# Level matmuls of the gated recurrence: 64 moving columns, one bank per chunk and level, two levels in four banks

## What is computed

```
def step(state, xs):                      # one chunk of 128 tokens
    qc, kc, vc, lfc = xs
    cb = jnp.cumsum(lfc, axis=1)
    rel = cb[:, :, None] - cb[:, None, :]
    dec = jnp.where(causal, jnp.exp(jnp.where(causal, rel, 0.0)), 0.0)
    a = jnp.einsum('bqhd,bkhd,bqkhd->bhqk', qc, kc, dec)
    o = jnp.einsum('bhqk,bkhe->bqhe', a, vc) + jnp.einsum('bqhd,bhde->bqhe', qc * jnp.exp(cb), state)
    ...
```

## Time and profile before

| | |
|---|---|
| time, median of 3 runs | 3101.59 us (3099.38 to 3101.69) |
| the profiled execution | 3100.82 us, its span 3099.0 us |
| TensorE's granted clock, mean over the span | 0.982 |
| TensorE busy | 95% of the span, 21052 matmul passes |
| weight loads busy | 86% |
| VectorE, ScalarE, GpSimd busy | 55%, 43%, 13% |

### The profile page before, as it was taken

The page is one execution under the profiler, slowest core; times in us unless marked ns, Lnnn a source line. Parts: engine busy times, 40 slices in busy tenths (PEclk is TensorE's granted clock), DMA queues, the critical chain, the costliest instruction groups (busy, mean ns, idle before and its releaser), DMA issues. The chain is left out here.

```text
span 3099.0 us, 54135 instructions
## 1 busy us (share of the span) xinstructions
PE 2951.6 (95%) x21052; PEld 2664.4 (86%) x21052; DVE 1717.1 (55%) x2483; ACT 1344.3 (43%) x1856; POOL 398.7 (13%) x306
## 2 busy tenths in 40 slices
PE   5999998999999999999899999999999998999998
PEld 2667765677999999899899989799999998988998
DVE  2223224276555556655445865657845577565784
ACT  1222213135544444544444544456644453536663
POOL 2111000122111110211100110101101002020110
PEclk8999999999999999999999999999999999999999
DMA  8986353841555654465435405245555451433564
GB/s 296 285 256 191 106 168 112 219 138 55 169 178 149 183 178 143 148 182 178 138 122 169 145 28 177 69 139 148 171 161 157 141 164 37 151 108 109 149 181 132
DMA packets 586161, 474.88 MB, mean 153 GB/s; under 512 B 28720, under 2 KB 547888, under 8 KB 585664
## 3 DMA queue, kind: packets, MB, share of 16 engines
q1 hardware_dynamic: 584464, 460.44, 48.7%
q0 software_dynamic: 1520, 11.95, 1.3%
HBM read 471.23 MB, written 4.72 MB: 154 GB/s over the span
## 5 line engine op out<-in xcount | busy, mean ns | idle before, releaser
L2213 DVE TENSOR_TENSOR low<-raw,high 128x1024 fp32r<-128x1024 f32 (+1 forms) x744 | 911.0, 1227 | 826.2 <-ACT high L2013 818.4
L2013 ACT CAST high<-raw 128x1024 fp32r<-128x1024 f32 (+1 forms) x744 | 767.9, 1033 | 1080.5 <-PE PS L1925 797.2
L1923 PE MATMUL PS<-NHh,high 128*128 128x272 f32 (+1 forms) x2304 | 669.2, 290 | 14.2 <-DVE NHl L1725 4.7
L1925 PE MATMUL PS<-NHh,low 128*128 128x272 f32 (+1 forms) x2304 | 661.1, 287 | 0.0
L1924 PE MATMUL PS<-NHl,high 128*128 128x272 f32 (+1 forms) x2304 | 660.2, 287 | 0.0
L1923 PE MATMUL PS<-XH,high 128*128 128x256 f32 (+1 forms) x1856 | 587.6, 317 | 28.3 <-issue 14.4
L1924 PE MATMUL PS<-XL,high 128*128 128x256 f32 (+1 forms) x1856 | 579.8, 312 | 0.0
L1925 PE MATMUL PS<-XH,low 128*128 128x256 f32 (+1 forms) x1856 | 579.6, 312 | 0.0
L1923 PEld LDWEIGHTS PS<-NHh,high 128*128 128x128 f32 x2304 | 433.4, 188 | 19.5 <-issue 15.4
L1924 PEld LDWEIGHTS PS<-NHl,high 128*128 128x128 f32 x2304 | 434.0, 188 | 0.8
L1925 PEld LDWEIGHTS PS<-NHh,low 128*128 128x128 f32 x2304 | 433.6, 188 | 0.0
(11 more groups left out here) (328 smaller groups left out, 4070.6 us busy)
## 6 DMA issues: line engine op xcount, KB each, us to landing
raw<-w_in_dram SPq DMA_DIRECT2D x416, 256.0 KB, 3.1
raw<-ffn_w_in_dram SPq DMA_DIRECT2D x352, 256.0 KB, 3.2
part<-ada_w_dram SPq DMA_DIRECT2D x184, 256.0 KB, 4.2
raw<-w_ffn_in_dram SPq DMA_DIRECT2D x176, 256.0 KB, 3.2
raw<-ffn_w_out_dram SPq DMA_DIRECT2D x160, 256.0 KB, 3.1
raw<-w_branch_dram SPq DMA_DIRECT2D x96, 256.0 KB, 3.2
raw<-w_ffn_out_dram SPq DMA_DIRECT2D x80, 256.0 KB, 3.0
part_sg<-ada_w_dram SPq DMA_DIRECT2D x48, 256.0 KB, 3.0
```

The lines of the kernel that those rows point to most:

```text
L1923: nc.tensor.matmul(out, wh, xh, start=(k0 + k == 0), stop=False)
L1925: last = nc.tensor.matmul(out, wl, xh, start=False, stop=(c == len(kch) - 1 and k == nk - 1))
L2013: nc.scalar.copy(high[:, slot, 0:nk, :], raw[:, slot, 0:nk, :]).then_inc(s_high, 1)
L2213: nc.vector.tensor_tensor(low[:, slot, 0:nk, :], raw[:, slot, 0:nk, :], high[:, slot, 0:nk, :].bitcast(F32), ALU.subtract).then_inc(s_low, 1)
```

## The change

A level's matmul keeps its 128 weight columns (all tokens of the chunk), but its moving operand is the right halves alone: `right_half(x, s)` takes s columns, leaves s out, and so on, 64 in all. The result is written without gaps, 64 values per head, so eight heads fill one bank of 512 values instead of two. Chunk c of level n now lies in bank 2 (n mod 2) + c: even levels in banks 0 and 1, odd levels in banks 2 and 3. So a chunk's bank was last used two levels below, and the wait on `s_hk` asks for the pick of chunk c of level n - 2 instead of n - 1. The pick reads its source without gaps and writes into `AM` as before. For the last chunk of 16 tokens the matmuls stay as they are, and the pick takes the right halves of what they wrote.

```diff
--- before.py
+++ after.py
@@ -1132,9 +1132,9 @@
                     last = nc.tensor.matmul(out, lhs[:, h, t0:t0 + wd], rhs[:, h, t0:t0 + wd], start=True, stop=True)
             return last
 
-        def level_banks(n, c):
-
-            return 2 * (c % 2)
+        def level_bank(n, c):
+
+            return 2 * (n % 2) + c
 
         def small_bank(n):
             return 4 if n % 2 else 5
@@ -1147,10 +1147,11 @@
                 for h in range(HH):
                     nc.tensor.matmul(PS[0:wd, small_bank(n), h * wd:(h + 1) * wd], q[:, h, t0:t0 + wd],
                                      q[:, h, t0:t0 + wd], start=True, stop=True)
-            t = slice(c * P, (c + 1) * P)
+            s, half = LEVELS[n], P // 2
             for h in range(HH):
-                last = nc.tensor.matmul(PS[:, level_banks(n, c) + h // 4, (h % 4) * P:(h % 4 + 1) * P],
-                                        q[:, h, t], q[:, h, t], start=True, stop=True)
+                x = q[:, h, c * P:(c + 1) * P]
+                out = PS[:, level_bank(n, c), h * half:(h + 1) * half].rearrange("p (b t) -> p b t", t=s)
+                last = nc.tensor.matmul(out, x, right_half(x, s), start=True, stop=True)
             return last
 
         def right_half(ap, s):
@@ -1171,7 +1172,7 @@
                     early(1)
                 pe.wait_ge(s_hq, NL * layer + n + 1)
                 for c in range(2):
-                    pe.wait_ge(s_hk, NPICK * layer + max(1, 2 * n + c))
+                    pe.wait_ge(s_hk, NPICK * layer + max(1, 2 * n + c - 2))
                     hg_level(n, c).then_inc(s_ht, 1)
             early(2)
             pe.wait_ge(s_hk, NPICK * (layer + 1))
@@ -1417,15 +1418,15 @@
                 dve.wait_ge(s_ht, t + 2 * n + c + 2)
                 dve.wait_ge(s_hk, NPICK * layer + 2 * n + c + 1)
                 s, m = LEVELS[n], C2["levels"] + (n + 1) * P
-                parts = [(c * P, P, PS[:, level_banks(n, c):level_banks(n, c) + 2, :])]
+                parts = [(c * P, P, PS[:, level_bank(n, c), :].rearrange("p (h b t) -> p h b t", h=HH, t=s))]
                 if c and s <= 8:
                     t0, wd = CHUNKS[2]
-                    parts.append((t0, wd, PS[0:wd, small_bank(n):small_bank(n) + 1, 0:HH * wd]))
+                    src = PS[0:wd, small_bank(n), 0:HH * wd].rearrange("p (h t) -> p h t", t=wd)
+                    parts.append((t0, wd, right_half(src, s)))
                 for t0, wd, src in parts:
-                    src = src.rearrange("p a (h t) -> p (a h) t", t=wd)
                     mask = con2[0:wd, m:m + wd].bitcast(I32)
                     last = nc.vector.copy_predicated(right_half(AM[0:wd, :, t0:t0 + wd], s),
-                                                     bc(right_half(mask, s), HH), right_half(src, s))
+                                                     bc(right_half(mask, s), HH), src)
                 last.then_inc(s_hk, 1)
 
             def end_exponents():
```

## The result

The changed kernel took 3117.18 us (median of 4 runs, 3115.23 to 3124.44), the kernel before 3101.16 beside it (4 runs, 3099.38 to 3101.69): ratio 1.0057, 95% interval 1.0039 to 1.0074. It is slower by 16 us, 2.6 times the 6.2 us (0.2%) that can be told from no change. The profiled run took 3115.23 with a span of 3113.4, 14.4 us over that of before.

What follows compares the result with a forecast made beforehand. TensorE (busy 95%) bounds the kernel, with levels 2 to 4 paced by GpSimd and VectorE. Profiled 3100.82 + 8.5 (layer 0) + 12.5 (layer 1) = 3121.8, given as 3122 us; own range 3113 to 3131, 8-in-10 range 3101 to 3131.

Steps and rivals of the forecast that it cites:

- The removed wait, worth nothing: Second chunk of a level no longer waits for the pick one level below; no TensorE wait named a pick: nothing.
- 64 columns gain TensorE nothing: Level matmuls: the weights' load sets the pace, so a 64-column pass stays at 0.1125 us at full clock.
- the third rival: Columns set the pace, about 0.06 us a pass, and the clock holds: 3.7 us gained per layer, 3093.4 us; chance 0.06.
- The strides at nothing: Level matmuls: reading the moving operand in strides was costed at nothing.
- Picks 0.5 us shorter on the path: Level 1's first pick, reading PSUM contiguously, gets shorter: -0.5 us per layer, bounds 0 and -0.6.
- The clock falls in levels 2 to 5 and comes back in the chunk after level 6: Each layer: TensorE drops to half clock somewhere in those levels, returning only in the merge-gate chunk after level 6.
- Price 0.22 a pass, 7.06 a level: At half clock a 64-column pass costs 0.22 us, and a level of 32 passes 7.06 us.
- Layer 0, +8.5: Layer 0 with the fall in mid level 3: +8.8 to the transposes, -1.3 in them, net +7.5; +8.5 taken.
- the 1.0 that I had added for an earlier fall: Layer 0: net +7.5 was raised to +8.5, as a fall one chunk earlier adds 2.0.
- Layer 1, +12.5: Layer 1: +4.0 for level 0 and its merge-gate chunk staying at half clock, plus layer 0's +8.5.
- then as in layer 0: Layer 1 after level 0 and its merge-gate chunk: the same +8.5 us as layer 0.
- a fall in level 5 alone, +2: Layer 0's sum: if the clock falls only in level 5, the loss is +2 us.

Runs made afterwards that it cites:

- the columns alone: Kernel before with only the level matmuls cut to 64 moving columns; its banks, wait and strided picks kept: 3116.93 us, ratio 1.0056.
- the half weights: Changed kernel with each level pass loading only 64 stationary columns, the second half of each block not computed: 3096.73 us (one run).
- the strides with 128 columns: Kernel before with level matmuls moving all 128 columns in strides, left blocks first, results placed as before: 3103.14 us, ratio 1.0001.

## Why the prediction was right, and where it was not

- *The bound.* Held. TensorE was the engine on whose time the result turned, and the pace of 4.86 us was set by GpSimd and VectorE until a level of TensorE's took longer.
- *The removed wait, worth nothing.* Held: the columns alone, with the wait in place, cost as much as the whole change.
- *64 columns gain TensorE nothing.* Held. At full clock 32 passes take 3.68 to 3.79 us against 3.84, at most 0.005 a pass, and the half weights show why: a pass of 0.068 us, near the third rival's 0.06, came only when the load was halved too. The Trainium skill's page "TensorE: Matmul & The Clock Gate", section "Back-to-back issue gap", gives by its isolated formula about half the time for half the columns; the measurement is 3.68 against 3.84, and it decides. The same section says that a stream of loads and matmuls is spaced by both; with that the traces agree: 0.119 us a pass on 64 moving columns with 128 weight columns, 0.068 with 64.
- *The strides at nothing.* Held, by the strides with 128 columns: 1.0001, at the pace that the weights' load sets.
- *Picks 0.5 us shorter on the path.* Wrong. They stayed at 1.30 to 1.32 at blocks of 1 and 2. The step that failed was the cause: I took the PSUM stride because operands strided in SBUF were not slow. That excluded strided SBUF for an ordinary VectorE operation, not for a predicated write. The text had named the alternative and its price, 1 us missing.
- *The clock falls in levels 2 to 5 and comes back in the chunk after level 6.* Held: 1799.55 to 1826.86 and 2611.92 to 2629.00, both ending within that chunk. In layer 0 the fall was in the second chunk of level 3, where the sum had it. The argument was weaker than it read: the stretch from 1829.50 that kept its clock "with few columns" also has four passes of 272 columns at 1837.84, and half clock can be left without such passes, as level 0 of layer 1 did before the change on passes of 128 columns and the half weights did after passes of 64.
- *Price 0.22 a pass, 7.06 a level.* Measured 6.83/32 = 0.213, so three levels cost 0.7 us less than the sum had.
- *Layer 0, +8.5.* Measured +10.6 to the transposes and -1.1 behind them (-1.3 forecast): +9.5. The agreement is in part luck. The levels from 3 on gave +8.1 of the +8.8 forecast, and the 1.0 that I had added for an earlier fall wasn't needed; but 3.1 us came at level 0's second chunk and the merge-gate chunk behind it, at half clock for 6.83 us, and the sum had that for layer 1 only. I had looked at where the clock was already low before the change, not at where the same few columns would bring it down afresh. The remaining -0.6 lies ahead of level 0, in the scores and the chunk behind them, which the change doesn't touch.
- *Layer 1, +12.5.* Measured +6.5, and -1.2 at the transposes: +5.3. Level 0 and its chunk were forecast at +4.0 and gave +1.5: +3.1 from the second chunk on, but the first chunk ran at full clock this time, -1.6. The fall came in level 5, not in level 3, and cost +5.0 where +8.8 stood. The columns alone had these two lengths the other way round, so the step that was mis-sized is "then as in layer 0". A fall two levels later was in the range, but the sum took the early one for both, and its figure for a fall in level 5 alone, +2, was itself too low: +5.0 and -1.2 at the transposes make +3.8.
- *Sum.* 3117.2 for 3122, in the forecast's own range; between the profiled runs 3115.2 for 3121.8. Layer 1 was sized 7.2 too high, layer 0 1.0 too low, and the rest of the program differs by 0.4. Of the 7.2, 3.1 is the place of the fall, 0.7 the price of the levels, 2.5 level 0 and its chunk, and 1.0 the allowance for an earlier fall. The place of the fall alone moves the end by some 3 us a layer: from level 0 to the transposes layer 0 lost 8.3 us with the columns alone, where it fell in level 5, and 11.2 with the whole change.

What stays open: what decides in which level the clock falls. Level 3 and level 5 both occurred, in the two layers of one execution, with the same code ahead of them. Nor is it shown what in these passes holds the clock down once it is down.

## What to carry to other kernels

Cutting the moving columns of a matmul pays only where they, and not the weights' load, set its pace; look for a row with still fewer columns behind the same load before you count on it. A TensorE that reads busy can be at half clock, stay there, as on these load-bound passes of few columns, and become the bound that it wasn't; so compare the clock's column over the stretch, and price a change of columns by what it does to the clock as well. Spare passes in a pause pay where the pause is certain; where it is not there, they stand in the way with their own length.

## What the hardware showed that was not expected

- Half clock lasted 27.3 us on 64-column passes with 128 weight columns, without one pause, and 3.4 to 6.8 us at a time on the same 64 columns with 64 weight columns and pauses of up to 2.75 us. From the busy share alone I would have expected the reverse.
- A pick (`copy_predicated`, 512 elements of 4 bytes) takes 1.31 us with its SBUF target in blocks of 1 or 2, and 0.73 with a contiguous one. The mask was strided in the pick of 0.73 too, and beside a strided target a strided PSUM source made no difference (1.31, 1.30 to 1.32 after). The Trainium skill's page "SBUF — State Buffer", section "Door 1: The DMA port swizzle (why `[64,N]` ≈ `[32,N]`)", says that PSUM lines hold two such values and that patterns which aren't contiguous are dear there, for matmuls. The trace doesn't bear this out for these: sixteen passes that wrote PSUM in strides took 2.09 us against 2.05, and the measurement decides; whether it would show on passes that no weights' load holds back, no run here tells.
